# One mixing product per head for both directions of a bidirectional state-space scan

## The reference

```python
seg = a_cum[:, :, :, None] - a_cum[:, :, None, :]
decay_ls = jnp.exp(jnp.where(lower, seg, -jnp.inf))
cb = jnp.einsum('bclgn,bcsgn->bclsg', cc, bc)
y_diag = jnp.einsum('bclsgr,bcsgrp->bclgrp', cb[..., None] * decay_ls, xdt)
y_off = jnp.einsum('bclgn,bcgrpn->bclgrp', cc, prev) * jnp.exp(a_cum)[..., None]
...
y = y_f + jnp.flip(y_b, 1) + xs * d_skip[:, None]
```

## Time and profile before

| | |
|---|---|
| median of three runs | 1921.04 us (1919.71 to 1922.29) |
| the profiled execution's own time | 1918.49 us |
| its span in the trace | 1916.7 us |
| TensorE matmul busy | 1671.8 us, 87% |
| VectorE busy | 1499.4 us, 78% |
| ScalarE busy | 593.6 us, 31% |
| POOL busy | 483.0 us, 25% |
| DMA from HBM | 346 GB/s over the span |

### The profile page before, as it was taken

The page is one execution under the profiler, slowest core; times in us unless marked ns, Lnnn a source line. Parts: engine busy times, 40 slices in busy tenths (PEclk is TensorE's granted clock), DMA queues, the critical chain, the costliest instruction groups (busy, mean ns, idle before and its releaser), DMA issues.

```text
span 1916.7 us, 18183 instructions
## 1 busy us (share of the span) xinstructions
PE 1671.8 (87%) x5422; PEld 924.0 (48%) x5422; DVE 1499.4 (78%) x3548; ACT 593.6 (31%) x1427; POOL 483.0 (25%) x516
## 2 busy tenths in 40 slices
PE   5999999998999887899898999879999987777776
PEld 5778468654554432333343677545444433232232
DVE  6899996767777767989887689787777778777755
ACT  2565672312223223323332111023222233322221
POOL 0000000023334333333343000033333333333341
PEclk9999999999999998999999999889999999999999
DMA  8333117979999999999999675679999999999996
GB/s 351 111 131 112 44 67 294 388 291 378 392 426 425 427 426 394 405 416 425 426 418 427 281 295 237 242 299 422 427 427 427 426 425 418 419 427 425 417 421 275
DMA packets 95186, 665.17 MB, mean 347 GB/s; under 512 B 11275, under 2 KB 13036, under 8 KB 15472
## 3 DMA queue, kind: packets, MB, share of 16 engines
q0 software_dynamic: 73728, 536.90, 67.3%
q1 hardware_dynamic: 21360, 127.11, 17.0%
HBM read 662.86 MB, written 1.11 MB: 346 GB/s over the span
## 4 chain that ended last, share of the span: by engine, by line
PE 43%; DMA 25%; DVE 23%; issue 4%; ACT 2%; PEld 1%; DVEq 0%; PEldq 0%; POOL 0%; SPq 0%; POOLq 0%; ACTq 0%
DMA expert_rows<-in_p_uv,chosen_experts 24%; PE bank L1055 20%; DVE dot_products L2223 6%; PE bank L1031 3%; PE bank L817 3%; PE bank L861 3%; PE bank L933 2%; DVE conv_work_or_state L1861 2%; DVE silu_c_row_and_products L1669 2%; PE bank L877 1%; PE bank L888 1%; PE bank L1249 1%; ACT weight_diagonal L1518 1%; PE bank L1176 1%; DMA hyena_weight_block<-in_h_in_blocks 1%
## 5 line engine op out<-in xcount | busy, mean ns | idle before, releaser
L1055 PE MATMUL bank<-expert_rows,weight_diagonal 128*128 128x512 f32 x2048 | 958.4, 611 | 173.2 <-ACT weight_diagonal L1518 172.5
L1289 POOL DMA_INDIRECT expert_rows<-in_p_uv,chosen_experts x512 | 482.8, 943 | 1407.3 <-PE bank L1055 784.2
L2223 DVE SCALAR_TENSOR_TENSOR dot_products<-expert_rows,bank 128x1024 f32<-128x1024 f32 x512 | 624.8, 1220 | 236.2 <-DMA expert_rows<-in_p_uv,chosen_experts 222.3
L1055 PEld LDWEIGHTS bank<-expert_rows,weight_diagonal 128*128 128x128 f32 x2048 | 380.1, 193 | 685.6 <-issue 388.2
L1518 ACT ACTIVATE weight_diagonal<-constants,expert_weights 128x128 f32<-128x128 f32 x512 | 177.8, 394 | 242.7 <-DVE expert_weights L2155 242.5
L1510 ACT ACTIVATE expert_gelu<-expert_dots 128x2 f32<-128x2 f32 x258 | 52.3, 203 | 608.5 <-DVE dot_products L2223 608.0
L817 PE MATMUL bank<-mixer_input_T_hi,weights_hi 128*128 128x512 f32 (+1 forms) x192 | 74.6, 388 | 22.0 <-DVE mixer_input_T_lo L1753 14.8
L1861 DVE SCALAR_TENSOR_TENSOR conv_work_or_state<-conv_work_or_state,channel_vectors 128x252 f32<-128x252 f32 (+1 forms) x192 | 82.4, 430 | 4.4
L1176 PE MATMUL bank<-hyena_input_T,hyena_weight_block 128*128 128x256 f32 x320 | 71.1, 380 | 4.4 <-DMA hyena_weight_block<-in_h_in_blocks 4.4
L817 PE MATMUL bank<-mixer_input_T_lo,weights_hi 128*128 128x512 f32 (+1 forms) x192 | 72.4, 377 | 0.0
L817 PE MATMUL bank<-mixer_input_T_hi,weights_lo 128*128 128x512 f32 (+1 forms) x192 | 72.2, 376 | 0.0
(11 more groups left out here) (298 smaller groups left out, 1921.9 us busy)
## 6 DMA issues: line engine op xcount, KB each, us to landing
weight_block<-in_ada_rows SPq DMA_DIRECT2D x24, 1024.0 KB, 6.0
weight_block<-in_m_in_blocks SPq DMA_DIRECT2D x20, 1024.0 KB, 5.0
hyena_weight_block<-in_ada_rows SPq DMA_DIRECT2D x16, 1024.0 KB, 5.4
hyena_weight_block<-in_h_in_blocks SPq DMA_DIRECT2D x12, 1024.0 KB, 7.2
weight_block<-in_wq_blocks SPq DMA_DIRECT2D x11, 1024.0 KB, 7.8
expert_rows<-in_p_uv,chosen_experts POOLq DMA_INDIRECT x512, 11.5
out_weights<-in_m_out_blocks SPq DMA_DIRECT2D x6, 1024.0 KB, 9.5
hyena_weight_block<-in_h_out_blocks SPq DMA_DIRECT2D x4, 1024.0 KB, 7.2
```

What stands on the lines that cost most here:

```text
L1055: last = mm(ps[b][:, :], dg[n % DIAG][:, :], uv[slot][:, D + h * 512:D + (h + 1) * 512], start=(r == 0 and k == 0), stop=end)
L1289: pool.indirect_dma_start(uv[slot][:, :], None, A[f"p_uv{l}"], bass.IndirectOffsetOnAxis(ap=chosen[:, s_, k:k + 1], axis=0)).then_inc(uv_l ...
L2223: stt(prod[:, :], uv[slot][:, 0:D], 1.0, rows_t, ALU.mult, ALU.mult, accum_out=dots[:, s_, k + j:k + j + 1]).then_inc(sem("dots_done"), 1)
```

## The change

The segment sums of both directions add up in one bank, since each is zero where the other counts; so there is one exponential for both and one mixing matmul for a head, with x itself as its right side. The steps dt go into C by B instead: for each head the lower triangle by the forward step plus the upper by the backward step. ScalarE makes the upper part of four heads of a round (`scale_cb`), VectorE that of the other four in one product (`cb_sides`), and VectorE adds the lower part to all eight, head by head (`both_sides`, one multiply-add each). C by B comes one round ahead. The skip term leaves `mixed` and goes to the z stage in eight pieces (`skip`): one before it, two in each of blocks 0, 1 and 2, and one in block 3, each piece 256 channels of both chunks. The output blocks are loaded in the order 0, 1, 4, 5, 2, 3, 6, 7, with a wait for all the pieces ahead of block 2.

```diff
@@ -51,6 +51,7 @@
+ACT_HEADS = 4
@@ -238,9 +239,9 @@
-    EM = [EM0, [btok[:, 2 * d:2 * d + 2, :].rearrange("p a b -> p (a b)").rearrange("p (h b) -> p h b", h=HPG) for d in range(2)]]
-    xdt = [[xw[j][:, d * GW:(d + 1) * GW] for d in range(2)] for j in range(2)]
-    cbm = hT[:, 6:8, 0:P]
+    EM = EM0
+    cbm = [hT[:, 6:8, j * P:(j + 1) * P] for j in range(2)]
+    cb_dt = [gate[j][:, :].rearrange("p (h b) -> p h b", h=HPG) for j in range(2)]
@@ -404,9 +405,8 @@
-            for d in range(2):
-                plan.use(("seg", c, g, d, 0), 4 + 2 * d)
-                plan.use(("seg", c, g, d, 1), 5 + 2 * d)
+            for h in range(2):
+                plan.use(("seg", c, g, h), 4 + 2 * (g % 2) + h)
@@ -659,11 +659,13 @@
-        sp.wait_ge(sem("scan_mixed"), 1)
-        for b in range(OUT_BLOCKS):
+        wait_read(sp, ("ydiag", 1, GROUPS - 1))
+        for n, b in enumerate((0, 1, 4, 5, 2, 3, 6, 7)):
+            if b == 2:
+                sp.wait_ge(sem("x_skipped"), 8)
             sp.dma_start(out_w[b], rows("m_out_blocks", b)).then_inc(sem(f"out_weights{b}_in"), 16)
-            if b + 3 < 8:
-                weights(at("z", b + 2) + 1, at("z", b + 3) + 1)
+            if n + 3 < 8:
+                weights(at("z", n + 2) + 1, at("z", n + 3) + 1)
@@ -870,13 +872,17 @@
                 if h == 0:
-                    pe.wait_ge(sem("x_dt"), 2 * i + 2)
-                    pe.wait_ge(sem("mixing_ready"), 2 * i + 2)
+                    pe.wait_ge(sem("mixing_ready"), i + 1)
                     b = begin(("ydiag", c, g))
-                for d in range(2):
-                    last = mm(ps[b][:, h * HD:(h + 1) * HD], EM[i % 2][d][:, h, :], xdt[i % 2][d][:, h * HD:(h + 1) * HD],
-                              start=(d == 0), stop=(d == 1))
+                x = xtok[:, 2 + c, g * GW + h * HD:g * GW + (h + 1) * HD]
+                last = mm(ps[b][:, h * HD:(h + 1) * HD], EM[i % 2][:, h, :], x, start=True, stop=True)
...
@@ -884,11 +890,15 @@
-                    b = begin(("seg", c, g, d, h))
-                    mm(ps[b][:, :], cst[:, (C_GT, C_LT)[d], :], aM[d][:, 4 * h:4 * h + 4, :].rearrange("p a b -> p (a b)"),
-                       start=True, stop=True).then_inc(full[b], 1)
-            b = begin(("cb", c, g))
-            mm(ps[b][:, 0:P], bcT[:, g, c * P:(c + 1) * P], ct_, start=True, stop=True).then_inc(full[b], 1)
+                    b = plan(("seg", c, g, h))[0] if d else begin(("seg", c, g, h))
+                    last = mm(ps[b][:, :], cst[:, (C_GT, C_LT)[d], :], aM[d][:, 4 * h:4 * h + 4, :].rearrange("p a b -> p (a b)"),
+                              start=(d == 0), stop=(d == 1))
+                    if d:
+                        last.then_inc(full[b], 1)
+            if i == 0:
+                cb_products(0)
+            if i + 1 < 2 * GROUPS:
+                cb_products(i + 1)
@@ -1402,22 +1412,33 @@
+        def scale_cb(i):
+            c, g = divmod(i, GROUPS)
+            wait_read(act, ("cb", c, g))
+            if i >= 2:
+                act.wait_ge(sem("mixing_ready"), i - 1)
+            for h in range(ACT_HEADS):
+                hh = HEADS + g * HPG + h
+                last = f(cb_dt[i % 2][:, h, :], cbm[i % 2][:, 1, :], ACT.Copy, scale=dt_t[:, 2 + c, hh:hh + 1])
+            last.then_inc(sem("cb_scaled"), 1)
...
+        scale_cb(0)
         for i in range(2 * GROUPS):
             c, g = divmod(i, GROUPS)
-            for d in range(2):
-                if i >= 2:
-                    wait_full(act, ("ydiag", *divmod(i - 2, GROUPS)))
-                elif i == 1:
-                    wait_full(act, ("S2", 1, GROUPS - 1))
-                for h in range(2):
-                    copy_out(("seg", c, g, d, h), EM[i % 2][d][:, 4 * h:4 * h + 4, :].rearrange("p a b -> p (a b)"), None, ACT.Exp)
+            if i >= 2:
+                wait_full(act, ("ydiag", *divmod(i - 2, GROUPS)))
+            for h in range(2):
+                copy_out(("seg", c, g, h), EM[i % 2][:, 4 * h:4 * h + 4, :].rearrange("p a b -> p (a b)"), None, ACT.Exp)
                 if i + 1 < 2 * GROUPS:
-                    mask_a(i + 1, d)
+                    mask_a(i + 1, h)
+            if i + 1 < 2 * GROUPS:
+                scale_cb(i + 1)
@@ -1895,36 +1916,41 @@
-            n = step(tt(heads(x), heads(x), bc(dskip[:, g * HPG:(g + 1) * HPG], HPG, HD), ALU.mult))
             tt(y, y, ps[b][:, :], ALU.add).then_inc(read[b], 1)
...
+        def both_sides(i, h0, h1):
+
+            c, g = divmod(i, GROUPS)
+            for h in range(h0, h1):
+                hh = g * HPG + h
+                n = step(stt(cb_dt[i % 2][:, h, :], cbm[i % 2][:, 0, :], dt_t[:, 2 + c, hh:hh + 1], cb_dt[i % 2][:, h, :], ALU.mult, ALU.add))
+            return n
+
+        def cb_sides(i):
+
+            c, g = divmod(i, GROUPS)
+            n = HPG - ACT_HEADS
+            w = dt_t[:, 2 + c, HEADS + g * HPG + ACT_HEADS:HEADS + (g + 1) * HPG]
+            after(step(tt(cb_dt[i % 2][:, ACT_HEADS:HPG, :], cbm[i % 2][:, 1, :].unsqueeze(1).to_broadcast([P, n, P]), bc(w, n, P), ALU.mult)))
+            both_sides(i, ACT_HEADS, HPG)
+
+        cb_masks(0)
+        cb_sides(0)
         for i in range(2 * GROUPS):
             c, g = divmod(i, GROUPS)
...
+            if i + 1 < 2 * GROUPS:
+                cb_masks(i + 1)
             y = yv[:, c, g * GW:(g + 1) * GW]
...
             n = step(tt(y, y, lnt[:, 0, :], ALU.add))
+            dve.wait_ge(sem("cb_scaled"), i + 1)
+            m = both_sides(i, 0, ACT_HEADS)
+            for h in range(2):
+                wait_read(dve, ("seg", c, g, h))
+            after(m)
+            tt(EM[i % 2][:, :, :], EM[i % 2][:, :, :], cb_dt[i % 2], ALU.mult).then_inc(sem("mixing_ready"), 1)
+            if i + 1 < 2 * GROUPS:
+                cb_sides(i + 1)
             modulation_dot(0, 2 * KD + i)
             after(n)
             if i:
                 mixed(i - 1)
         mixed(2 * GROUPS - 1)
+
+        def skip(j0, j1):
+
+            for j in range(j0, j1):
+                x, y = (w[:, :, j * BLK:(j + 1) * BLK] for w in (xtok[:, 2:4, :], yv))
+                d = dskip[:, 4 * j:4 * j + 4].unsqueeze(1).unsqueeze(3).to_broadcast([P, TT, 4, HD])
+                x4 = x.rearrange("p t (h d) -> p t h d", h=4)
+                after(step(tt(x4, x4, d, ALU.mult)))
+                tt(y, y, x, ALU.add).then_inc(sem("x_skipped"), 1)
...
+        skip(0, 1)
...
         for j in range(8):
             wait_read(dve, ("z", j))
             y = yv[:, :, j * BLK:(j + 1) * BLK]
+            dve.wait_ge(sem("x_skipped"), j + 1)
             tt(y, y, zs[j % 2].rearrange("p (t c) -> p t c", t=TT), ALU.mult).then_inc(sem("y_gated"), 1)
...
+            skip(min(8, 2 * j + 1), min(8, 2 * j + 3))
```

More of the change, by code:

```diff
@@ L1897, in mixed, with cb_masks @@
             c, g = divmod(i, GROUPS)
-            y, x = yv[:, c, g * GW:(g + 1) * GW], xtok[:, 2 + c, g * GW:(g + 1) * GW]
+            y = yv[:, c, g * GW:(g + 1) * GW]
             b = wait_full(dve, ("ydiag", c, g))
-            n = step(tt(heads(x), heads(x), bc(dskip[:, g * HPG:(g + 1) * HPG], HPG, HD), ALU.mult))
             tt(y, y, ps[b][:, :], ALU.add).then_inc(read[b], 1)
-            after(n)
-            wait_read(dve, ("ydiag", c, g))
-            last = tt(y, y, x, ALU.add)
-            if i == 2 * GROUPS - 1:
-                last.then_inc(sem("scan_mixed"), 1)
-                dve.wait_ge(sem("scan_mixed"), 1)
-            else:
-                step(last)
+        def cb_masks(i):
+            c, g = divmod(i, GROUPS)
+            b = wait_full(dve, ("cb", c, g))
+            n = step(tt(cbm[i % 2][:, 0, :], ps[b][:, 0:P], cst[:, C_LE, :], ALU.mult))
+            tt(cbm[i % 2][:, 1, :], ps[b][:, 0:P], cst[:, C_GE, :], ALU.mult).then_inc(read[b], 1)
+            after(n)
+            wait_read(dve, ("cb", c, g))
@@ L1919, in _ @@
-            n = step(tt(cbm[:, 0, :], ps[b][:, 0:P], cst[:, C_LE, :], ALU.mult))
-            tt(cbm[:, 1, :], ps[b][:, 0:P], cst[:, C_GE, :], ALU.mult).then_inc(read[b], 1)
-            after(n)
-            wait_read(dve, ("cb", c, g))
-            for d in range(2):
-                for h in range(2):
-                    wait_read(dve, ("seg", c, g, d, h))
-                e = EM[i % 2][d]
-                tt(e[:, :, :], e[:, :, :], cbm[:, d, :].unsqueeze(1).to_broadcast([P, HPG, P]), ALU.mult).then_inc(sem("mixing_ready"), 1)
+            if i + 1 < 2 * GROUPS:
+                cb_masks(i + 1)
@@ L1941, in _ @@
         mixed(2 * GROUPS - 1)
+        def skip(j0, j1):
[5 more added lines that the diff above has]
+                tt(y, y, x, ALU.add).then_inc(sem("x_skipped"), 1)
+        for g in (GROUPS - 2, GROUPS - 1):
+            wait_read(dve, ("ydiag", 1, g))
+        skip(0, 1)
         modulation_bias(0, 2)
```

11 lines of the change are left out of this document (5 added, 6 removed).

## The result

| | before | after |
|---|---|---|
| median | 1921.07 us (8 runs, 1919.71 to 1923.0) | 1927.62 us (8 runs, 1925.66 to 1933.61) |
| ratio | | 1.0031, 95% interval 1.0019 to 1.0042 |
| the profiled execution's own time | 1918.49 us | 1933.61 us |

The kernel became slower by 0.31%. That is inside the range of 1917 to 1929, near its upper end, and past the 0.2% that the prediction took as no change: not the case of the highest chance, but the next one. The profiled execution lies 6.0 us above the median. In the traces the stage of the experts, which no edit touches, differs by about as much: from its first combination (the first matmul with the experts' rows) to the end it takes 1491.9 us before and 1499.2 after. So I compare stretches inside the trace, and leave that stage out. The first combination starts 7.75 us later (424.83 before, 432.58 after).

The account below looks back on a forecast made before the run. VectorE and TensorE both set the scan's end, VectorE alone after the change. Scan -2.1, clock +1.7, gate diagonal +3.4 sum to +3.0 us: 1924.0 from a median of 1921.04, range 1917 to 1929.

Parts of the forecast that it names:

- the case of the highest chance: Whole kernel: no change, within about 0.2% (3.8 us) of the kernel before; chance 0.51.
- the next one: Whole kernel: slower, by a second clock fall or dearer multiply-adds; chance 0.37.
- rival d: Scan: TensorE's saving is paid out, VectorE's round under 7.2 us; 10.7 us faster, 1910.3; chance 0.12.
- rival b: Scan, VectorE: multiply-adds go at a pace of 0.32, 64 on the path; +3.2 us, 1927.2; chance 0.09.
- two passes: Scan, VectorE: multiply-adds at two passes a column, 0.40 each; +11.5 us, 1932.5; chance 0.03.
- The wait at the gate diagonal: Z stage: skip pieces make the diagonal end 3.52 us late, so TensorE waits 3.4 us ahead of its gate rows.
- rival (a): Gate diagonal: the clock falls a second time in the 3.4 us wait; price 1.7, sum +4.7, 1925.7; chance 0.25.
- Both lie under VectorE's round below, so I cost them at nothing: Scan, ScalarE: its 6.8 us of work and 7.0 us mask loop a round are covered by VectorE's 8.54; cost nothing.
- the later fall: Scan's end: TensorE's idling likely takes the clock to 1.2 GHz; 1.7 us lost.
- the loop through a matmul: Scan, ScalarE: 16 masks, two exponentials and one matmul with its way back, 7.0 us a round.
- about 5 us at the last: Scan: TensorE, paced by VectorE, stands idle about 5 us ahead of the last mixing.
- The queues: Z stage loads: SP's wait costs nothing; the z block asked for 1.4 us later lands during TensorE's new wait.

Follow-up runs that it names:

- e8: Changed kernel with the skip term back in the scan's rounds and no skip pieces in the z stage: 1933.32 us, ratio 1.0058.
- e9: The kernel of e1, unchanged, profiled and timed again: 1926.08 us, ratio 1.0014.
- e3: Changed kernel with round 0's scaled copies behind its exponentials and the gate diagonal ahead of z block 0: 1924.23 us, ratio 1.0017.
- e4: e3 plus all eight parts of the first z product ahead of the last mixing: 1921.40 us, ratio 0.9994.
- e5: e4 plus mixings alternating between banks 3 and 6, first z product in bank 7: 1917.63 us, ratio 0.9970.
- e10: Kernel before with only the skip term moved beside z and SP's new order, directions kept apart: 1929.0 us, ratio 1.0030.
- e6: e5 plus each z block's modulation dots ahead of its skip pieces, gate diagonal behind block 0's dots: 1917.67 us, ratio 0.9966.
- e1: Changed kernel with ScalarE's first scaled copies moved behind both exponentials of round 0: 1927.27 us, ratio 1.0036.

## Why the prediction was right, and where it was wrong

**Held.** VectorE became the bound of the scan: 8.50 us a round for 8.54, the multiply-adds 0.26 for 0.27 apiece. TensorE's 14.1 us were not paid out (rival d), and e8 shows the converse: with 1.4 us more a round on VectorE the kernel loses. The price of 0.32 (rival b) and that of two passes are out. For the latter the Trainium skill's sentence (Vector Engine (DVE) Microarchitecture Reference, section 7) was set against the dot's row, and the row was right: the 64 multiply-adds took 0.346 each, 0.26 from start to start, and not the 0.40 of two passes. The wait at the gate diagonal came, 2.81 for 3.4; the skip pieces are 1.33 each, since the wait behind a 128x512 multiply costs 0.72 from start to start, not 0.78. The clock fell behind it, rival (a), 1.84 for 1.7; as e9 shows it need not have. The wait for z block 3's weights was also seen: its load was asked for 1.6 us later after the scan's end than before (8.61 for 6.99), for 1.4 in the forecast, and landed during the stall.

**The step that failed is ScalarE at the scan's start**: "Both lie under VectorE's round below, so I cost them at nothing", and "so no table load comes". That compared a steady round with a steady round. At the start there is no round to hide under: the copies stand in order ahead of the exponential, their wait and the table load went onto the path, and the last product ended at 293.4 instead of 290.3. Without the copies ahead (e3, e4, e5) it ended 70.1 to 70.2 us after the first sum, just the 70.2 of the forecast. Of the 3.1 us, 1.4 are the wait itself and 1.7 a fall of the clock behind it, which the forecast did not have either. With 0.3 of the price of the later fall (2.0 for 1.7) that makes the 3.4 us by which the scan came out late against the sum. Besides, the 7.0 for the loop through a matmul is a slip: 16 x 0.29 + 2 x 0.48 + 1.2 is 6.8. Nothing hung on it.

**The five idle microseconds were not there.** The text expected TensorE to wait "about 5 us at the last" mixing. It idled 1.11 or 1.33 a round and 0.39 there, as it was held earlier by the bank. I had looked for the data that a mixing needs, not for the reader of the bank that it writes. The clock fell nevertheless: the term was right in size, its reason not. At the scan's end it fell behind idle times of 1.1 to 1.3 a round, while 3.35 us left it at 1.00 in e8, and 3.11 at 431.54 in the kernel before. By the Trainium skill (TensorE: Matmul & The Clock Gate, Part 1) idleness lowers it and activity restores it; the runs agree in that the kernel before, with a full TensorE, had no fall in the scan and each profile of a changed one has, save e10, where TensorE is full too. The place is not fixed by the program: in two executions of one the clock fell at different places. So what was costed as one certain term is a chance of 2 us at each of several places.

**The queues** were costed at nothing, as the load was to land during TensorE's wait. In after that was so: 1.6 us of waiting for weights showed once the stall was gone (e3), and vanished with the dots moved ahead (e6).

**The sum** was -2.1 + 1.7 + 3.4 = +3.0. By the trace it is -0.7 (the scan without clock losses, with 1.4 of ScalarE's start in it) + 1.7 (clock at the start) + 2.0 (clock at the scan's end) + 2.8 (wait at the gate rows) + 1.8 (clock behind it) = +7.6; the timed difference is +6.5. Where the 1.1 between them comes from was not tried.

**Luck.** The time fell inside the range by luck in part. The upper bound, 1928.9, left 3.2 us for a slow multiply-add (b) that did not come, and nothing for ScalarE's start and the fall behind it, which cost 3.1. Three falls of the clock were met where one was in the sum and a second had a chance of 0.25.

## What to carry to other kernels

Merging two products into one saves on the engine that multiplies and charges the one that prepares the operand; cost the round of every engine, and the first round by itself, since what waits in an in-order queue there hides under nothing. For each matmul that waits, ask for the last reader of its bank as well as for its data: here a second bank for the mixing was worth 3.6 us in the trace and 3.8 at the median (e5 below e4), with not one instruction less. And when a stall goes, look in the same place for the transfer that it covered.

## What was not expected of the hardware

The granted clock of one program differs from execution to execution in place: 0.89 or 1.00 in the window from 130 to 145 us, with the same instructions, and in the scan 0.84 in one profile and 1.00 in the other (284 to 305 us, e1 and e9). In the scan and at the gate rows a fall cost 1.3 (e9 at 241 us), 1.7 (after at 232), 1.8 and 2.0 us. It came behind idle times of 1.1 to 1.3 us and stayed away behind 3.35. One kernel's ratio moved by up to 0.22% (4 us) from one set of eight to ten runs to the next, so a smaller difference between kernels of this length needs more runs than ten.
